# A two-block transformer kernel: the tail of block two by token tile, and the first expert block ahead of the expert loop

## The reference

```python
x = _layernorm(ALPHA * x + g1 * (mixed[:, CTX_LEN:] @ w_out[l]), ln1_g[l], ln1_b[l])
ffn = _hier_moe(_modulate(x, sh2, sc2), rt_g[l], rt_g_b[l], rt_e[l], rt_e_b[l], ex_gate[l], ex_up[l], ex_down[l])
x = _layernorm(ALPHA * x + g2 * ffn, ln2_g[l], ln2_b[l])
...
def _hier_moe(h, rt_g, rt_g_b, rt_e, rt_e_b, ex_gate, ex_up, ex_down):
    ...
    # each token picks one of 4 groups, and the best 2 of the 8 experts in it
    ...
    def expert_block(args):
        idx, w, e = args
        xb = tok_pad[idx]
        hb = jax.nn.silu(xb @ ex_gate[e]) * (xb @ ex_up[e])
        return (hb @ ex_down[e]) * w[:, None]
```

## Time and profile before

| | |
|---|---|
| median of 3 runs | 2342.2 us (2337.0 to 2344.39) |
| profiled execution, its own time | 2340.76 us |
| its span | 2338.9 us |
| mean granted TensorE clock | 0.957 of full |
| PE busy | 2142.5 us (92%) |
| DVE, ACT, POOL busy | 827.6, 504.6, 244.9 us |
| DMA | 392.93 MB, mean 168 GB/s over the span |
| expert loop in the span | from about 1834 to 2316 us |

### The profile page before, as it was taken

How to read it: one execution, slowest core, us unless ns; L and a number is a source line. 1 busy time by engine, 2 the same in 40 slices (tenths; PEclk the granted TensorE clock), 3 DMA queues, 4 the chain that set the end, 5 groups by cost and what they waited for, 6 DMA issues and landing times.

```text
span 2338.9 us, 36872 instructions
## 1 busy us (share of the span) xinstructions
PE 2142.5 (92%) x15185; PEld 1415.3 (61%) x15185; DVE 827.6 (35%) x1534; ACT 504.6 (22%) x880; POOL 244.9 (10%) x221
## 2 busy tenths in 40 slices
PE   8989999998999999996999798699997799999995
PEld 5777778845777868852245455599964344444442
DVE  1377220002378220003048825534445222222224
ACT  2254000001354200000132123343321111111111
POOL 1376000000457000000000001000000000000000
PEclk9999999999999999998999898799997899999998
DMA  7431544435432444444712120000041699999993
GB/s 221 144 107 60 212 135 154 144 126 168 144 108 90 180 141 148 144 150 151 262 50 84 60 72 1 2 4 4 4 156 46 286 423 403 401 401 401 400 402 128
DMA packets 139384, 392.93 MB, mean 168 GB/s; under 512 B 16967, under 2 KB 64431, under 8 KB 127729
## 3 DMA queue, kind: packets, MB, share of 16 engines
q1 hardware_dynamic: 139249, 390.95, 45.0%
HBM read 389.88 MB, written 1.05 MB: 167 GB/s over the span
## 4 chain that ended last, share of the span: by engine, by line
PE 44%; DVE 5%; ACT 1%; DMA 1%; issue 1%; SPq 0%; POOL 0%; DVEq 0%; ACTq 0%; POOLq 0%
PE psum L1225 9%; PE psum L2536 9%; PE psum L1883 6%; PE psum L2560 5%; PE psum L1932 3%; PE psum L1249 2%; PE psum L2517 2%; PE psum L2587 2%; PE psum L1398 2%; PE psum L1911 1%; PE psum L2229 1%; DMA arena<-in_ex_up_dram 1%; PE psum L2548 1%; PE psum L2215 1%; DVE arena L1844 1%
## 5 line engine op out<-in xcount | busy, mean ns | idle before, releaser
L364 PE MATMUL psum<-arena,ring 128*128 128x256 f32 x1728 | 390.2, 386 | 17.2 <-DVE arena L935 15.9
L364 PEld LDWEIGHTS psum<-arena,ring 128*128 128x128 f32 x1728 | 330.7, 193 | 73.8 <-issue 16.6
L573 PE MATMUL psum<-arena,ring 128*128 128x256 f32 (+1 forms) x1536 | 306.8, 361 | 3.2 <-ACT arena L624 3.2
L573 PEld LDWEIGHTS psum<-arena,ring 128*128 128x128 f32 x1536 | 270.5, 189 | 39.3 <-ACT arena L624 4.1
L624 ACT ACTIVATE arena<-psum 128x512 f32<-128x512 f32 (+2 forms) x116 | 62.9, 567 | 544.4 <-PE psum L573 264.0
L1883 PE MATMUL psum<-arena 64*64 64x64 f32 (+1 forms) x3808 | 149.0, 228 | 20.6 <-DVE arena L2060 18.1
L1883 PEld LDWEIGHTS psum<-arena 64*64 64x64 f32 x3808 | 139.4, 136 | 23.3 <-DVE arena L2060 18.8
L600 PE MATMUL psum<-ring,arena 128*128 128x512 f32 x352 | 151.4, 592 | 0.0
L1225 PE MATMUL psum<-arena,ring 128*128 128x512 f32 (+2 forms) x432 | 143.0, 491 | 0.0
L1225 PEld LDWEIGHTS psum<-arena,ring 128*128 128x128 f32 (+1 forms) x432 | 81.3, 189 | 62.2 <-issue 56.4
L1013 DVE TENSOR_TENSOR arena<-arena,psum 128x512 f32<-128x512 f32 x22 | 15.2, 690 | 288.8 <-PE psum L573 288.8
(11 more groups left out here) (378 smaller groups left out, 2638.6 us busy)
## 6 DMA issues: line engine op xcount, KB each, us to landing
ring<-in_w_in_dram SPq DMA_DIRECT2D x31, 2048.0 KB, 8.2
ring<-in_ffn_w_dram SPq DMA_DIRECT2D x46, 1024.0 KB, 7.0
ring<-in_ex_gate_dram SPq DMA_DIRECT2D x15, 2048.0 KB, 10.6
ring<-in_ex_up_dram SPq DMA_DIRECT2D x15, 2048.0 KB, 15.1
ring<-in_ex_down_dram SPq DMA_DIRECT2D x15, 2048.0 KB, 7.5
arena<-in_ex_gate_dram SPq DMA_DIRECT2D x15, 2048.0 KB, 11.1
arena<-in_ex_up_dram SPq DMA_DIRECT2D x15, 2048.0 KB, 15.6
arena<-in_ex_down_dram SPq DMA_DIRECT2D x15, 2048.0 KB, 17.4
```

The source lines that it names most:

```text
L364: ins = pe.matmul(bank[:, j, :], w[:, kc, c * P:(c + 1) * P], moving[:, kc, :], start=kc == 0, stop=kc == k - 1)
L573: ins = pe.matmul(bank[:, j, tokens], both[:, i * DC + kc, j * P:(j + 1) * P], K.xT[:, kc, tokens], start=kc == 0, stop=kc == DC - 1)
```

## The change

1. **Tail by token tile.** The `w_out` products run token tile by token tile; those of tile 0 begin with the four chunks of `mixed` that are there early, and the rest waits for one piece of `mixed` at a time. The head normalisation and what follows it are done head pair by head pair. The layer norms, the transposes and the router products of tile 0 come before those of tile 1; layer norm has two passes over a tile in place of three. One half of the `g2` row is made before the choices are counted, the other half after it, and the transposes back move behind the counting. Small transfers are issued nearer to their use, the first half of `w_out` earlier.
2. **First expert block apart.** `route` of tile 0 writes token 0's first expert into `block_expert`. SP loads this expert's three matrices into the arena buffers of `j` = 1 as soon as the number is known. `plan` takes one block off that expert (`its`), so that the loop has one block fewer, and this block is computed ahead of the loop (`xg1`, `in1`, `hidT1`, `down1`, `put1`).
3. **Gate row at the output of down.** `gated_output` multiplies the down product by the `g2` row while it takes it out of PSUM, both halves on DVE; ACT's copy L2612 goes. The residual is added by the first block's put, so that `acc` needs no memset and `finish_vector` is statistics and layer norm, each token tile with a transfer of its own.

```diff
 def tail_sync(sp, K, A):
...
+    for unit in tail_units()[0:3]:
+        weights(*unit)
+    sp.wait_ge(K.sem["c_rows"], K.count("c_rows"))
...
+    weights(*tail_units()[5])
+    sp.wait_ge(K.sem["mixed_r"], K.count("mixed_r"))
+    sp.wait_ge(K.sem["first_expert"], K.count("first_expert"))
+    e = sp.value_load(K.block_expert[0:1, 2 * PAIRS + 1:2 * PAIRS + 2], min_val=0, max_val=EXPERTS - 1)
+    for unit, sources in (("in", (A["ex_gate_2"], A["ex_up_2"])), ("down", (A["ex_down_2"],))):
+        for a, dst in zip(sources, K.pair_w["pair_" + unit, 1]):
+            k = a.shape[2] // P
+            part = a[0, bass.ds(e, 1)].rearrange("a (p k) n -> p (a k) n", k=k)
+            sp.dma_start(dst.rearrange("p (k n) -> p k n", k=k), part).then_inc(K.landed(("one_" + unit, 0)), 16)
...
 def tail_tensor(pe, K):
...
+    def out_product(tt, hf, kcs):
...
+        for kc in kcs:
+            if kc >= DC // 2:
+                pe.wait_ge(K.sem["mixed_r"], K.count("mixed_r", 0, kc - DC // 2 + 1))
...
+    for tt in range(TT):
+        token_tile_turned(tt)
+        router_products(tt)
+    gate_rows("g2", (10, 11), (0,))
...
+    for tt in range(TT):
+        for hf in range(2):
+            pe.wait_ge(K.empty(("h2", tt, hf)), K.empty_count(("h2", tt, hf)))
...
+    gate_rows("g2", (10, 11), (1,))
...
 def tail_scalar(act, K):
...
-    for tt in range(TT):
         act.wait_ge(K.sem["x4_var"], K.count("x4_var", 0, tt + 1))
         act.activation(K.x_std2[:, tt:tt + 1], K.x_mv2[:, tt, 1:2], ACT.Sqrt).then_inc(K.sem["x4_std"], 1)
...
+        for i in range(2):
+            q = 2 * tt + i
+            act.wait_ge(K.full(("h2T", q)), K.full_count(("h2T", q)))
...
+    if tt == 0:
+        n = 2 * PAIRS + 1
+        ts_op(K.owner[:, n:n + 1], s[:, 3:4], -1.0, float(EXPERTS), ALU.mult, ALU.add).then_inc(link.sem, 1)
+        dve.wait_ge(link.sem, link.count())
+        dve.tensor_copy(K.block_expert[:, n:n + 1], K.owner[:, n:n + 1]).then_inc(K.sem["first_expert"], 1)
...
+    tt_op(blocks, blocks, its, ALU.subtract).then_inc(link.sem, 1)
...
+                if (unit, j) == ("pair_down", 0):
+                    sp.wait_ge(K.full(("g2", 1)), K.full_count(("g2", 1)))
...
+    pe.wait_ge(K.sem["one_chosen"], K.count("one_chosen"))
...
+    pe.wait_ge(K.landed(("one_in", 0)), K.landed_count(("one_in", 0)))
...
+    pe.wait_ge(K.sem["one_hid"], K.count("one_hid"))
...
+    pe.wait_ge(K.landed(("one_down", 0)), K.landed_count(("one_down", 0)))
...
-        def out_low(j):
-
-            act.wait_ge(K.full(("down", j)), K.full_count(("down", j), i))
-            act.activation(K.p_out[j * PLACES:(j + 1) * PLACES, 0, :], K.bank(("down", j))[0:PLACES, :], ACT.Copy).then_inc(
-                K.sem["out_low"], 1)
...
+def gated_output(dve, K, j, hf, bank):
+
+    part = slice(hf * PLACES, (hf + 1) * PLACES)
+    return dve.tensor_tensor(K.p_out[j * PLACES:(j + 1) * PLACES, hf, :], bank[part, :],
+                             K.g_rows[part, 1, hf * BANK:(hf + 1) * BANK], ALU.mult)
...
+            dve.scalar_tensor_tensor(out=K.acc[:, tt, part], in0=K.x_tok[:, tt, part], scalar=ALPHA_2, in1=K.bank(key),
+                                     op0=ALU.mult, op1=ALU.add).then_inc(K.empty(key), 1)
...
-            dve.tensor_copy(K.p_out[j * PLACES:(j + 1) * PLACES, 1, :], K.bank(("down", j))[PLACES:P, :]).then_inc(K.sem["out_high"], 1)
+            for hf, name in enumerate(("out_low", "out_high")):
+                gated_output(dve, K, j, hf, K.bank(("down", j))).then_inc(K.sem[name], 1)
...
 def finish_vector(dve, K):
     link = Chain(K.dve_done, K.dve_base)
     for tt in range(TT):
-        dve.tensor_tensor(K.acc[:, tt, :], K.acc[:, tt, :], K.g_rows[:, 1, :], ALU.mult).then_inc(link.sem, 1)
-        dve.wait_ge(link.sem, link.count())
-        x = K.x_tok[:, tt, :]
-        dve.scalar_tensor_tensor(out=x, in0=x, scalar=ALPHA_2, in1=K.acc[:, tt, :], op0=ALU.mult, op1=ALU.add).then_inc(link.sem, 1)
-        dve.wait_ge(link.sem, link.count())
-        row_stats(dve, K, link, x, tt, "x5_var")
-    layer_norm_2(dve, K, link, "x5", 2, "x5")
+        row_stats(dve, K, link, K.acc[:, tt, :], tt, "x5_var")
+        layer_norm_2(dve, K, link, "x5", 2, tt, K.acc[:, tt, :]).then_inc(K.sem["x5"], 1)
```

More of the change, by code:

```diff
@@ L51 @@
 W2_ROWS = 4
-DMAS = {"w13": 2, "pair_in": 2}
+DMAS = {"w13": 2, "pair_in": 2, "one_in": 2}
 PAIR_SLOTS = 4
@@ L2445, in plan @@
         dve.wait_ge(K.full(("pos", tt)), K.full_count(("pos", tt)))
-    total = K.bank(("pos", 1))[:, EXPERTS:2 * EXPERTS]
-    blocks, ends, first = (K.plan[:, k, :] for k in range(3))
+    total, its = (K.bank(("pos", 1))[:, k * EXPERTS:(k + 1) * EXPERTS] for k in (1, 2))
+    blocks, ends, first, apart = (K.plan[:, k, :] for k in range(4))
     ts_op(blocks, total, 0.0, None, ALU.is_gt).then_inc(link.sem, 1)
@@ L2989, in _ @@
             pair_sync(sp, K, A)
[L2990 to L2992 removed]
+            for tt in range(TT):
+                sp.wait_ge(K.sem["x5"], K.count("x5", 0, tt + 1))
+                sp.dma_start(out[0, tt * P:(tt + 1) * P, :], K.x_tok[:, tt, :]).then_inc(K.dma_out, 16)
+            sp.wait_ge(K.dma_out, 32)
         @block.gpsimd
```

371 lines of the change are left out of this document (232 added, 139 removed).

## The result

The changed kernel took 2306.5 us in the median of four runs (2304.6 to 2310.3), beside 2343.3 us (2337.0 to 2345.2) for the kernel before: a ratio of 0.985, 95% interval 0.9827 to 0.9873. The forecast was 2302 in a range of 2293 to 2315, so the time lies inside it, 4.5 us above its centre. In a second series of five runs the median was 2305.0 (ratio 0.9846, 0.9829 to 0.9863). The profiled execution took 2304.61 us with a span of 2302.9, 36.0 less than the span before.

The account below looks back on a forecast made before the run. TensorE was taken to set the pace, transfers 5% behind. From 2340.8 us, -31.2 - 6.3 + 3.9 - 6.0 + 0.8 - 0.8 = -39.6 gave 2301.2; the predicted median was 2302, range 2293 to 2315.

Parts of the forecast that it names:

- The pair and the routing: In the loop: counts make 29 blocks, one is taken out, 14 pairs run instead of 15; minus 31.2 us.
- The kept pair: Rival, in the loop: routing gives 30 blocks, so 15 pairs run behind the first block; 2333.5 us, chance 0.03.
- The loop's start: Ahead of the loop: its start moves from 1846.3 to 1840, minus 6.3 us.
- `planned` at 1802.0: Ahead of the loop: the plan reaches `planned` at 1802.0, 26 us earlier than before; after 1808 would show the prediction wrong.
- The first block from 1808.5 on, 31.5 us: Ahead of the loop: TensorE starts the first block at 1808.5; its steps take 30.7 us, loop start taken as 1840.
- half clock through the first block: Rival, ahead of the loop: waits cut TensorE's stream, so half clock; start 1846 to 1850, 2308 to 2312 us, chance 0.15.
- TensorE never waiting for a DMA from 1786 on: Sign, ahead of the loop: weights of the first block and first pair arrive before TensorE needs them.
- The period: In the loop: each pair takes 0.3 us more, period 31.5 us; plus 3.9 us over 13 periods.
- `choose` and the sums begin one instruction later: At a pair's seam, on DVE: they begin 2.2 us after the puts' start, not 1.44; with two sums 3.8 us.
- The finish: After the loop: 9.7 us instead of 15.7, minus 6.0 us.
- The last transfer: At the end: half as large, taking 3.2 us between bounds of 2.0 and 4.0; minus 0.8 us.
- Slower than before: Rival, at a pair's seam: later `choose` and sums hold the next pair; from 34.6 us a period on, chance 0.02.

Follow-up runs that it names:

- experiment 1: Changed kernel with the counted blocks raised from 28 to 29, so the loop takes a 15th, empty pair: 2332.45 us.
- experiment 3: Changed kernel with its third part undone: outputs copied plainly by ACT and DVE, gate row and residual applied at the end: 2303.75 us, ratio 0.9854.
- experiment 5: Kernel of experiment 4, with PE's waits for the second block's output weights and bank moved ahead of the transposes of the places: 2291.66 us, ratio 0.9793.
- experiment 6: Changed kernel with loops of 14 trips instead of 20 on every engine, right for this input alone: 2296.0 us.
- experiment 8: Kernel of experiment 5, with DVE's loop cut into 14 trips and a second loop skipped as a whole: ratio 0.9798, runs 2286.4 to 2300.2 us.
- the repeated kernel: The changed kernel run again without any edit, five runs: 2299.3 to 2310.0 us.
- experiment 4: Changed kernel with DVE's place shift and choice of the next pair's rows moved between the two outputs: ratio 0.9819.
- experiment 2: Changed kernel without the first block computed ahead; all 29 blocks counted in 15 pairs, tail and gate row kept: 2318.08 us.
- experiment 7: Changed kernel with unused matmuls in PE's idle stretches: ten, four and three, 2309.74 us; with five, two and one, median 2305.5 us.
- the last run of experiment 8: Kernel of experiment 8 with five, two and one unused matmuls added in PE's idle stretches: 2292.35 us, ratio 0.9793.

## Why the prediction was right, and where it was not

**The pair and the routing.** Right. 14 puts and one ahead of the loop; the fifteenth pair, put back, cost 31.1 us from the loop's start on. The kept pair as a rival is excluded: the puts of pairs in the changed kernel run from 1867.34 to 2280.20, which is 13 periods of 31.76.

**The loop's start.** Right in sum (1840 forecast, 1839.6), by two errors that cancelled in this execution. *`planned` at 1802.0* was 4 us early here: the output products began at 1745.5, not 1744.8, and took 29.4, since the clock fell to 0.72 near their start, not 27.4; and the half of the `g2` rows took 9.12 us in place of 8.6. In six of seven other profiled executions with the same instructions up to here (experiments 1, 3, 5, 6, 8 and the repeated kernel) the products began at 1742.0 to 1744.6 and took 27.7, and the cast stood at 1800.6 to 1802.8, as worked out. In the seventh, experiment 4's, they began at 1750.3 and the cast stood at 1809.9, behind the 1808 that was named as a sign of being wrong. So one and the same work ends anywhere in a stretch of 9 us, and that `planned` stayed under 1808 in the profiled execution was partly luck. *The first block from 1808.5 on, 31.5 us*, was too dear: 27.95 (1811.68 to 1839.63), mostly because the clock stayed at 1.00. I had taken the pair's gather at 5.0, between its two levels, gate and up at 7.8, output products at 4.3 and the small gather at 3.9; at full clock they are 3.84, 7.0, 3.66 and 3.79, together 2.7 less. Another 0.8 is that my terms add to 1839.2 and I took 1840. At a low clock the block takes 32.1 and 35.3 us (the profiles of experiments 4 and 3), so the rival *half clock through the first block* is real and comes in some executions: it is a part of the width of the range, not another centre. Its reason, that waits cut PE's stream into pieces, is not shown: the waits were the same 1.84 and 1.30 us in the execution at full clock.

**"TensorE never waiting for a DMA from 1786 on".** Right. The weights of the first block were issued at 1789.1, and neither they nor the first pair's were waited for. Without the block both waits came back (experiment 2).

**The period.** The term that was most off in size. The mechanism was named (*`choose` and the sums begin one instruction later*) and so was its row, DVE's sums. Forecast were 0.3 us a pair; 0.53 were measured, 6.9 us in place of 3.9, still inside the bound of 0.6 that I gave. The early choice removes 0.45 of it, so this much was the wait for the sums. With the row's numbers the sum would have come out: put start to first sum is 2.21 us (2026.13 to 2028.34), two sums with their gap are 1.56, and the release takes some 0.28 more before PE's next product, 4.05 in all; I had left out the release and set 3.8. The other 0.1 is not the term that I had named, the output's first half being ready 0.1 later: the puts start 0.82 us after the products, where it was 0.86 before. (Against experiment 3's 0.73 the multiplication does cost 0.1; against the kernel before it does not show.) It is PE's gap ahead of the second block's output products, 0.29 in place of 0.15, which comes with the first block (experiment 2 has 0.15) and goes with the waits ahead (experiment 5). The prediction says that a pair has one gap; it had this second one too.

**Leaving the loop.** Missed. The row was on the table, has "[3.01 <-issue]", and I read it as a fixed price. It is the trips that are left over: a pair fewer is a skipped trip more (0.7 us), and a trip costs more than before, which is the other 0.8. In the kernel before and in the one without the first block, five trips took 3.01 and 3.04 us, in the changed kernel with five trips 3.83. The dearer trip comes with the first block and not with the gate row, since experiment 2 has the gate row and 3.04, and experiment 3 lacks it and has 4.66 for six. What in the loop it changes was not tried and stays open.

**The finish.** Right: 9.8 against 9.7. What the forecast did not put side by side is that its 6 us and the seam's 6.9 are the two sides of one edit, which comes out at nothing or slightly below (experiment 3).

**The last transfer.** 512 KB landed in 2.6 us, where I took 3.2 between bounds of 2.0 and 4.0, and the end came 1.4 us nearer, not 0.8. The Trainium skill's fit ("DMA: Bandwidth & Descriptors", section "Anatomy of one DMA") also gave 3.2 and is 0.6 us above this store, which SP issues.

**Slower than before.** Nothing near: it needed a period of 34.6, and 31.76 was measured.

## What to carry to other kernels

Where work is counted in whole pairs of blocks, ask which count the input gives and whether one block can be moved off it: the block apart cost 15 us and bought a pair of 31.6. By the same count it would pay only where the rest becomes an even number, as here, where 29 blocks became 28; no other input was run. When an instruction moves to an engine that is idle on average, add up what that engine does between the last product of an iteration and the release on which the next one waits; here five small instructions, 1.3 us in all, stood in that stretch, and putting them one step earlier gave back 5.8 us. Short gaps without a clear releaser are worth an experiment each. Of two looked at here, one, put down to "issue", was six empty trips of a loop (4.2 us) and the other register work of waits that could stand earlier (0.2 us a pair), although the profile named an ACT copy as its releaser.

## What the runs showed of the hardware

- **A trip of a loop whose body is skipped is not free.** 0.70 us on DVE (4.53, 3.83 and 0.30 us with six, five and no skipped trips); a branch over the whole rest left a gap of 0.51.
- **The clock differs between executions of one program.** The first block's gather of 32 small matmuls took 3.79 us at a granted clock of 1.00 and 6.28 to 6.84 at a lower one, after much the same gate rows and the same idle 1.84 us. Work put into PE's idle stretches was followed by 4 us at a clock of 1.00 in one trace (experiment 7, five fillers), and then by 0.57; it did not move the centre of the times. What decides it stays open.
- **An f32 matmul of the code stands twice in the trace, the kernel's own too.** The 32 output products are x64 and took 27.70 us at full clock, 0.43 a record and 0.87 for one of the code. Ten unused ones, counted as x20, took 10.53 us at a clock of 0.74 to 1.00; five took 4.54 us at 1.00 in the last run of experiment 8, 0.91 each. Whoever prices an added matmul at the 0.43 of one record is too low by half.
